# Making the first pair of token blocks with eight plain block products while the weights' sums are made, in a one-core hybrid pooling and attention block

## The chip, the cores and the metric

One core of one Trainium2 chip runs the whole block. The metric is the device time of one execution in microseconds (us). TensorE (PE) multiplies, VectorE (DVE), ScalarE (ACT) and GpSimd (POOL) do the elementwise work, and SyncE (SP) issues the DMAs.

## The reference

For 4096 tokens of width 1024 the block computes the following. The part that this change is about is the first line and the products with the columns of `w_in` that make v (attention values) and the attention gate.

```python
h = rms_norm(x, norm_gain)                       # (4096, 1024)
proj = h @ w_in                                  # (1024, 3072): pool_v, pool_g, q, k, v, attn_g
y_pool = multiscale_pool(pool_v, pool_w, pool_scale) * silu(pool_g)
y_attn = chunked_rel_attention(q, k, v, rel_bias) * silu(attn_g)
x = x + concat(y_pool, y_attn) @ w_out
out = rms_norm(x, final_norm_gain)
```

## The kernel before

The program has three phases that follow one another on every engine: the h phase (`h_phase_pe` and its sisters), the q phase (pool path and queries and keys) and the a phase (attention and output). The change lies in the h phase.

The h phase takes the 32 blocks of 128 tokens in 16 pairs p = 0 to 15. For each block it loads x, squares it (ACT, `square`), takes the root (POOL, `rstd`), normalises it (DVE, `normalise`) and transposes it on PE (`transposes(n)`, n = 2p or 2p+1, eight matmuls of 128x128 fp32). Every fp32 operand and every weight is split into two f16 parts, a high one made by ACT (`operand_hi`, `sum_hi`, `weight_hi`) and a low one, the rest, made by DVE (`operand_lo`, `weight_lo`) or, for sums of operands, by POOL (`sum_lo`). A pair times the 1024x1024 weights (columns of v and of the gate) is a product of 2x2 blocks of matrices. It is done with seven block products instead of eight (a Strassen-like scheme): `product(p, s)`, s = 0 to 6, twelve matmuls of 128x512 f16 each. The price is sums: four sums of operands per pair (DVE, `sums`), and, once, four sums of the weight quadrants W11, W12, W21, W22. DVE makes these four in halves of 128x1024 fp32 (`weight_s1`, `weight_sum`), and seven weights are split in halves (`weight_hi`, `weight_lo`), so product 1 can't start until DVE has summed, ACT has made the high part and DVE the low part. The results are taken out of PSUM by DVE (`take_u2`, `take_u4`, `take_c22`, `take_c12`, `take_c21`, `take_c11_lo`) and ACT (`copy_p1`, `v11_hi`), and stored.

The order of instructions on each engine is written out by hand: a list for the first pair(s) and then a loop over p. All engines issue in order, so an instruction that waits holds up everything behind it on its engine. In the loop, DVE does `take_c21(p - 1)` and `normalise(2p + 2)` first, and PE does `transposes(2p + 2)` after product 1 of pair p. In the four pairs of `FOLD_AT` PE does extra work beside the products (`fold_transposes`, `fold_products`): it folds the small pool weights into columns of w_in. In the pair after each, ACT, DVE and POOL split the folded weights (`group_hi`, `group_lo`, `group_sums`). In pair 3 DVE also makes the rows of the bias (`bias_rows`).

Of the kernel before, what the change touches and what calls it, by code (L numbers as in the profile page):

```python
# [65 lines left out]
FOLD_AT = (1, 4, 7, 10)  # L66
# [33 lines left out]
def build(nc, x, norm_gain, w_in, pool_w, pool_scale, rel_fwd, rel_rev, w_out, final_gain, out):  # L100
# [13 lines left out]
    with ctx:  # L114
# [3 lines left out]
        def sem(name):  # L118
# [90 lines left out]
        names = """ident0 ident_ready consts log_ready inv_ready ones_ready gain_loaded pw_loaded small_loaded  # L209
            w_hi w_lo s1_done sum_done wst_loaded fold_t fold_copied fold_mm fold_done fs_done  # L210
            ss_done ms_done rstd_done xn_done tr_done hhi_done hlo_done b12_done t_done th_done tl_done h_stored
# [6 lines left out]
        z_stored = [sem(f"h_z_stored{s}") for s in range(2)]  # L218

        def h_phase_pe(pe):  # L220
# [48 lines left out]

            def product(p, s):  # L270

                if p == 0:
                    pe.wait_ge(H["w_lo"], 2 * s + 2)
# [3 lines left out]
                if s == 0:  # L277
                    at_least(pe, H["c11_lo"], p)
                elif s < 4:
                    at_least(pe, H["u_done"], 5 * (p - 1) + (1, 4, 5)[s - 1])  # L280
                elif s == 4:
                    pe.wait_ge(H["p1_done"], p + 1)
                else:
                    pe.wait_ge(H["u_done"], 5 * p + s - 3)
# [11 lines left out]
            transposes(1)  # L296
            for p in range(PAIRS):
                for s in range(PRODUCTS):
# [9 lines left out]
                    elif p + 1 < PAIRS:  # L308
                        if s == (4 if p == 0 else 1):
                            transposes(2 * p + 2)  # L310
                        if s == (5 if p == 0 else 3):
                            transposes(2 * p + 3)
# [8 lines left out]
        def w_source(s, half):  # L321

            kts = slice(2 * half, 2 * half + 2)
            return (wraw[:, 0, kts, :], wsum[:, 1, kts, :], wsum[:, 0, kts, :], wsum[:, 2, kts, :], wraw[:, 1, kts, :],
                    wsum[:, 0, kts, :], wraw[:, 3, kts, :])[s]

        def h_phase_act(act):
# [11 lines left out]
            def weight_hi(s, half):  # L339

                if s in (0, 4, 6):
                    act.wait_ge(wraw_loaded[2 * {0: 0, 4: 1, 6: 3}[s] + half], 16)
                elif s == 2:
                    act.wait_ge(H["s1_done"], half + 1)
                else:
                    act.wait_ge(H["sum_done"], {1: 0, 3: 2, 5: 4}[s] + half + 1)
                nc.scalar.activation(wvg[:, s, 0, 2 * half:2 * half + 2, :], w_source(s, half), ACT.Copy,
                                     scale=WS).then_inc(H["w_hi"], 1)

# [14 lines left out]
            def sum_hi(p, i):  # L364

                act.wait_ge(H["t_done"], 4 * p + i + 1)
                nc.scalar.activation(hop1[:, p % 2, (2, 1, 3, 6)[i], 0, :], tsum[:, i, :], ACT.Copy).then_inc(H["th_done"], 1)

            def copy_p1(p):
                act.wait_ge(H["prod_mm"], PRODUCTS * p + 1)  # L370
                at_least(act, H["u_done"], 5 * (p - 1) + 1)
                nc.scalar.activation(u1[:, 0, :], pj[0][:, :], ACT.Copy, scale=1 / WS).then_inc(H["p1_done"], 1)

            def v11_hi(p):
                act.wait_ge(H["prod_mm"], PRODUCTS * p + 5)
# [7 lines left out]
            def v12_hi(p):  # L383
                act.wait_ge(H["u_done"], 5 * p + 4)
# [5 lines left out]
            def gate_tanh(p, e):  # L390

                act.wait_ge(H["u_done"], 5 * p + (3 if e else 5))
# [15 lines left out]
            def group_hi(i, j):  # L408

                s, src = parts_of_group(j)  # L410
                if j == 0:
                    act.wait_ge(H["w_lo"], 14)
                    if i == GROUPS - 1:
                        act.wait_ge(H["ext_stored"], 16)
# [7 lines left out]
            weight_hi(0, 1)  # L422
            operand_hi(0, 0)
            operand_hi(0, 1)
            copy_b12(0)
            operand_hi(0, 2)
            sum_hi(0, 0)
            sum_hi(0, 1)
            weight_hi(1, 0)
            weight_hi(1, 1)  # L430
            sum_hi(0, 2)
            sum_hi(0, 3)
            weight_hi(2, 0)
            weight_hi(2, 1)
            copy_p1(0)
            weight_hi(3, 0)
            weight_hi(3, 1)
            square(2)
            weight_hi(4, 0)
            weight_hi(4, 1)  # L440
            square(3)
            weight_hi(5, 0)
            weight_hi(5, 1)
            weight_hi(6, 0)
            weight_hi(6, 1)
            v11_hi(0)
            operand_hi(1, 0)
            operand_hi(1, 1)
            square(4)
            copy_b12(1)  # L450
            operand_hi(1, 2)
            for i in range(4):
                sum_hi(1, i)
            gate_tanh(0, 1)
            square(5)
            v12_hi(0)
# [37 lines left out]
        def h_phase_dve(dve):  # L494
# [3 lines left out]
            def weight_s1(half):  # L498

                kts = slice(2 * half, 2 * half + 2)  # L500
                dve.wait_ge(wraw_loaded[4 + half], 16)
                dve.wait_ge(wraw_loaded[6 + half], 16)
                nc.vector.tensor_tensor(wsum[:, 0, kts, :], wraw[:, 2, kts, :], wraw[:, 3, kts, :],
                                        ALU.add).then_inc(H["s1_done"], 1)

            def weight_sum(which, half):

                kts = slice(2 * half, 2 * half + 2)
                a11, a12, a21 = wraw[:, 0, kts, :], wraw[:, 1, kts, :], wraw[:, 2, kts, :]
                if which == 2:  # L510
                    dve.wait_ge(wraw_loaded[half], 16)
                    dve.wait_ge(H["s1_done"], half + 1)
                    ins = nc.vector.tensor_tensor(wsum[:, 1, kts, :], wsum[:, 0, kts, :], a11, ALU.subtract)
                elif which == 3:
                    ins = nc.vector.tensor_tensor(wsum[:, 2, kts, :], a11, a21, ALU.subtract)
                else:
                    dve.wait_ge(wraw_loaded[2 + half], 16)
                    dve.wait_ge(H["sum_done"], half + 1)
                    dve.wait_ge(H["w_lo"], 4 + half + 1)
                    ins = nc.vector.tensor_tensor(wsum[:, 0, kts, :], a12, wsum[:, 1, kts, :], ALU.subtract)  # L520
                ins.then_inc(H["sum_done"], 1)

            def weight_lo(s, half):
                dve.wait_ge(H["w_hi"], 2 * s + half + 1)
                nc.vector.scalar_tensor_tensor(  # L525
                    out=wvg[:, s, 1, 2 * half:2 * half + 2, :], in0=w_source(s, half), scalar=WS,
                    in1=wvg[:, s, 0, 2 * half:2 * half + 2, :], op0=ALU.mult, op1=ALU.subtract).then_inc(H["w_lo"], 1)

# [37 lines left out]
            def take_u2(p):  # L566
                dve.wait_ge(H["prod_mm"], PRODUCTS * p + 2)
                dve.wait_ge(H["p1_done"], p + 1)
                at_least(dve, H["u_done"], 5 * p)
                combine(u1[:, 1, :], pj[1], u1[:, 0, :])  # L570

            def take_u4(p):
                dve.wait_ge(H["prod_mm"], PRODUCTS * p + 3)
                dve.wait_ge(H["u_done"], 5 * p + 1)
                combine(u1[:, 2, :], pj[2], u1[:, 1, :])

            def take_c22(p):
                dve.wait_ge(H["prod_mm"], PRODUCTS * p + 4)
                dve.wait_ge(H["u_done"], 5 * p + 2)
# [28 lines left out]
            def group_lo(i, j):  # L608
                s, src = parts_of_group(j)
                dve.wait_ge(H["w_hi"], 14 + 7 * i + j + 1)  # L610
# [4 lines left out]
            def bias_rows():  # L615
# [5 lines left out]
                dve.wait_ge(H["w_lo"], 14)  # L621
# [10 lines left out]
            weight_lo(0, 0)  # L632
            normalise(1)
            weight_lo(0, 1)
            operand_lo(0, 0)
            operand_lo(0, 1)
            sums(0)
            operand_lo(0, 2)
            for half in range(2):
                weight_s1(half)  # L640
                weight_sum(2, half)
            for s in (1, 2):
                weight_lo(s, 0)
                weight_lo(s, 1)
            for half in range(2):
                weight_sum(3, half)
            take_u2(0)
            weight_lo(3, 0)
            weight_lo(3, 1)
            take_u4(0)  # L650
            weight_lo(4, 0)
            weight_lo(4, 1)
            for half in range(2):
                weight_sum(4, half)
            normalise(2)
            weight_lo(5, 0)
            take_c22(0)
            weight_lo(5, 1)
            normalise(3)
            weight_lo(6, 0)  # L660
            weight_lo(6, 1)
            take_c11_lo(0)
            operand_lo(1, 0)
# [1552 lines left out]
```

## Time and profile before

| | |
|---|---|
| time, median of 3 runs | 1685.61 us (1684.76 to 1685.9) |
| the profiled execution's own time | 1687.45 us |
| its span, first to last instruction | 1685.7 us |
| PE busy | 1618.0 us (96%) |
| DVE, ACT, POOL busy | 1064.6, 835.5, 691.8 us |
| mean granted TensorE clock | 0.988 of full |

The span is what the trace shows. The h phase fills about its first 365 us. "Busy" of PE counts overlapping matmuls, so two matmuls that start 0.2 us apart and take 0.38 us each show as continuous work.

### The profile page before, as it was taken

How to read it: one execution, taken by the hardware profiler on the slowest of the kernel's cores; microseconds unless marked ns; L12 is line 12 of the kernel's file. 1: busy time of each engine (PE TensorE's matmuls, PEld its weight loads, DVE VectorE, ACT ScalarE, POOL GpSimd, SP SyncE). 2: the span in 40 equal slices, each digit the busy share in tenths (PEclk: the TensorE clock that was granted, in tenths of full speed). 3: DMA queues.
4: the chain of work that ended last, by engine and by line, in shares of the span. 5: the costliest groups of instructions: out<-in, count | busy, mean ns of one | idle time of the engine just before them, and what ended most of it. 6: DMA issues, size and time to landing. Idle time of an engine off the chain costs nothing. (4 is left out here: it accounts for less than half of the span.)

```text
span 1685.7 us, 44263 instructions
## 1 busy us (share of the span) xinstructions
PE 1618.0 (96%) x17920; PEld 1219.7 (72%) x17920; DVE 1064.6 (63%) x2188; ACT 835.5 (50%) x1580; POOL 691.8 (41%) x734
## 2 busy tenths in 40 slices
PE   4999999999999999999988999999999999999986
PEld 2545545558677776777767888889888899888864
DVE  7777677647565566557346666666666666666664
ACT  5655555422121111112125677767777767777674
POOL 2545445311101111112413555555555555555553
PEclk8999999999999999999998999999999999999998
DMA  5564664564524532452854524444334444344331
GB/s 212 204 232 166 202 234 162 216 245 150 212 68 172 198 147 79 176 189 98 232 186 131 154 85 134 139 141 140 119 103 133 146 139 144 87 134 132 104 123 51
DMA packets 131201, 257.87 MB, mean 153 GB/s; under 512 B 15512, under 2 KB 61096, under 8 KB 128952
## 3 DMA queue, kind: packets, MB, share of 16 engines
q1 hardware_dynamic: 129960, 253.74, 44.7%
q8 instruction: 143, 2.34, 0.6%
q0 software_dynamic: 1040, 1.31, 0.4%
q14 instruction: 58, 0.48, 0.1%
HBM read 151.33 MB, written 83.48 MB: 139 GB/s over the span
## 5 line engine op out<-in xcount | busy, mean ns | idle before, releaser
L2092 POOL TENSOR_TENSOR stages<-stages 128x512 f16<-128x512 f32 (+2 forms) x368 | 364.0, 991 | 366.4 <-ACT stages L1929 366.2
L1561 PE MATMUL bank<-middle,weights 128*128 128x128 f16 x1792 | 313.2, 220 | 2.1 <-DVE entry L1208 0.9
L1564 PE MATMUL bank<-middle,weights 128*128 128x128 f16 x1792 | 313.1, 220 | 0.0
L1563 PE MATMUL bank<-middle,weights 128*128 128x128 f16 x1792 | 313.0, 220 | 0.0
L1923 ACT ACTIVATE stages<-bank,log_ps 128x512 f32<-128x512 f32 (+2 forms) x368 | 221.6, 602 | 161.9 <-PE bank L1816 97.0
L1763 DVE CUSTOM_DVE_ANT_0 stages<-bank,stages 128x640 bf16<-128x640 f32 (+4 forms) x256 | 198.7, 776 | 76.0 <-PE bank L1728 75.8
L977 PE MATMUL bank<-middle 128*128 128x256 f16 x784 | 213.7, 273 | 3.7 <-DVE stages L1117 3.7
L979 PE MATMUL bank<-middle 128*128 128x256 f16 x784 | 213.7, 273 | 0.0
L980 PE MATMUL bank<-middle 128*128 128x256 f16 x784 | 213.7, 273 | 0.0
L1929 ACT ACTIVATE stages<-stages 128x512 f16<-128x512 f32 (+2 forms) x368 | 202.8, 551 | 11.7
L1793 PE MATMUL bank<-entry,stages 128*128 128x512 f16 x768 | 193.3, 383 | 2.5 <-DVE stages L1984 2.5
L289 PE MATMUL bank<-weights,middle 128*128 128x512 f16 x448 | 172.2, 384 | 10.3 <-DVE weights L525 10.3
L1561 PEld LDWEIGHTS bank<-middle,weights 128*128 128x128 f16 x1792 | 176.1, 98 | 3.3 <-issue 1.3
L1563 PEld LDWEIGHTS bank<-middle,weights 128*128 128x128 f16 x1792 | 176.2, 98 | 0.4
L1564 PEld LDWEIGHTS bank<-middle,weights 128*128 128x128 f16 x1792 | 176.2, 98 | 0.0
L292 PE MATMUL bank<-weights,middle 128*128 128x512 f16 x448 | 171.8, 383 | 0.0
L291 PE MATMUL bank<-weights,middle 128*128 128x512 f16 x448 | 171.6, 383 | 0.0
L1001 PE MATMUL bank<-entry,stages 128*128 128x512 f16 x768 | 171.3, 382 | 0.0
L1813 PE MATMUL bank<-middle 128*128 128x256 f16 (+1 forms) x840 | 162.4, 243 | 2.8 <-DVE middle L2016 1.6
L1283 POOL TENSOR_TENSOR stages<-stages 128x512 f16<-128x512 f32 x32 | 38.2, 1194 | 300.0 <-ACT stages L1062 300.0
L1001 PEld LDWEIGHTS bank<-entry,stages 128*128 128x128 f16 x768 | 75.3, 98 | 86.7 <-issue 2.3
L1594 DVE SCALAR_TENSOR_TENSOR middle<-bank,middle 128x256 f32<-128x256 f32 x160 | 67.8, 424 | 103.2 <-PE bank L1564 102.0
(147 smaller groups left out, 3613.0 us busy)
## 6 DMA issues: line engine op xcount, KB each, us to landing
entry<-in_x SPq DMA_DIRECT2D x64, 512.0 KB, 3.7
h_ops<-middle SPq DMA_DIRECT2D x16, 1792.0 KB, 6.1
middle<-h_ops SPq DMA_DIRECT2D x112, 256.0 KB, 6.0
middle<-h_ops SPq DMA_DIRECT2D x49, 512.0 KB, 7.1
middle<-middle SPq DMA_DIRECT2D x384, 64.0 KB, 2.0
residual<-entry SPq DMA_DIRECT2D x32, 512.0 KB, 2.8
entry<-residual SPq DMA_DIRECT2D x30, 512.0 KB, 5.4
out<-entry SPq DMA_DIRECT2D x30, 512.0 KB, 2.6
```

The source lines that it names most:

```text
L977: nc.tensor.matmul(bank, wh, hop[:, :, s, 0, kt, :], start=(kt == 0 and s < 4), stop=False, skip_group_check=True)
L979: nc.tensor.matmul(bank, wh, hop[:, :, s, 1, kt, :], start=False, stop=False, skip_group_check=True)
L980: mm = nc.tensor.matmul(bank, wl, hop[:, :, s, 0, kt, :], start=False, stop=(kt == 3), skip_group_check=True)
L1001: mm = nc.tensor.matmul(op_bank(n, n2), part, w[:, kt, n2 * 512:(n2 + 1) * 512], start=(kt == 0 and w is wot_h and part is yh), stop=(kt = ...
L1561: nc.tensor.matmul(dst, wh, hop3[:, o, 0, kt, :], start=(kt == 0 and s < 2 and pair == 0), stop=False, skip_group_check=True)
L1563: nc.tensor.matmul(dst, wh, hop3[:, o, 1, kt, :], start=False, stop=False, skip_group_check=True)
L1564: mm = nc.tensor.matmul(dst, wl, hop3[:, o, 0, kt, :], start=False, stop=(kt == 3), skip_group_check=True)
L1763: nc.vector.tensor_tensor_reduce((junk0 if t == 0 and h < 2 else junk2)[:, c:640], wide[:, c:640], bias_q[:, h, c:640], 1.0, -3e38, ALU.ad ...
L1793: mm = nc.tensor.matmul(out_bank(t, i), yh, w, start=(m == 0), stop=(m == 11))
L1923: nc.scalar.activation(p32[g][:, a:b], score_bank(g)[:, a:b], ACT.Exp, bias=log_ps[:, 0:1]).then_inc(A["exp_done"], 1)
L1929: nc.scalar.activation(p_h[:, h % 2, c + a:c + b], p32[g][:, a:b], ACT.Copy).then_inc(A["ph_done"], 1)
L2092: nc.gpsimd.tensor_tensor(p_l[:, h % 2, c + a:c + b], p32[g][:, a:b], p_h[:, h % 2, c + a:c + b], ALU.subtract).then_inc(A["pl_done"], 1)
```

## The change

The first pair (p = 0) no longer uses the sums. It is made by eight products of plain quadrants (`FIRST`: weight, place of the operand, PSUM bank), two into each of four banks. The quadrants are put where splits 0, 4, 5 and 6 of the seven lie (`WSPLITS`); split 5 is overwritten later by its sum. Each bank then holds a result, which DVE takes out with one multiplication (`first_take`). The sums are made in the meantime and are needed from pair 1 on: two of them (W21+W22 and W11-W21, two halves each) by POOL instead of DVE, the other two by DVE. Eight weights are split instead of seven. The second operand quadrant of block 0 gets a split of its own (`first_b12_hi`, `first_b12_lo`). Transposes 1, 2 and 3 stand among the eight products. The gain is loaded before the first weights, W12 before W21 and W22. Everything of pair 1's operands and of the second, third and fourth normalise stands at new places in the lists. The folds move from pairs 1, 4, 7, 10 to 2, 5, 8, 11, and with them the splits from pairs 2, 5, 8, 11 to 3, 6, 9, 12; `bias_rows` stays in pair 3. The first columns of the folded group are loaded after the stores of pair 0.

```diff
-FOLD_AT = (1, 4, 7, 10)
+FIRST = ((0, 0, 0), (1, 4, 0), (0, 6, 1), (1, 5, 1), (2, 0, 2), (3, 4, 2), (2, 6, 3), (3, 5, 3))
+WSPLITS = (0, 4, 5, 6, 1, 2, 3, 5)
+FOLD_AT = (2, 5, 8, 11)
...
+            def first_product(q):
+                w, place_, role = FIRST[q]
+                if place_ == 6:
+                    pe.wait_ge(H["b12_lo"], 1)
+                else:
+                    pe.wait_ge(H["hlo_done"], {0: 1, 4: 2, 5: 3}[place_])
+                for kt in range(4):
+                    if kt % 2 == 0:
+                        pe.wait_ge(H["w_lo"], 2 * w + kt // 2 + 1)
...
             def product(p, s):
-                if p == 0:
-                    pe.wait_ge(H["w_lo"], 2 * s + 2)
+                if p == 1 and s in (1, 2, 3, 5):
+                    pe.wait_ge(H["w_lo"], {1: 10, 2: 12, 3: 14, 5: 16}[s])
...
             transposes(0)
-            transposes(1)
-            for p in range(PAIRS):
+            for q in range(len(FIRST)):
+                first_product(q)
+                if q == 0:
+                    transposes(1)
+                if q == 5:
+                    transposes(2)
+                if q == 6:
+                    transposes(3)
+            for p in range(1, PAIRS):
...
             def weight_hi(w, half):
+                if w == 7:
+                    act.wait_ge(H["prod_mm"], 6)
+                    act.wait_ge(H["w_lo"], 6)
...
+            def first_take(which):
+                dve.wait_ge(H["prod_mm"], 2 * which + 1)
+                nc.vector.tensor_scalar(cs1[:, which - 1, :], pj[which][:, :], 1 / WS, None,
+                                        ALU.mult).then_inc(H["u_done"], 1)
...
+            for half in range(2):
+                weight_sum(7, half)
+                weight_lo(7, half)
             gate_z(0, 1)
-            take_c12(0)
...
+            def weight_sum(w, half):            # POOL
+                kts = slice(2 * half, 2 * half + 2)
+                pool.wait_ge(wraw_loaded[4 + half], 16)
+                if w == 5:
+                    pool.wait_ge(wraw_loaded[6 + half], 16)
+                    ins = nc.gpsimd.tensor_tensor(wsum[:, 0, kts, :], wraw[:, 2, kts, :], wraw[:, 3, kts, :], ALU.add)
+                else:
+                    pool.wait_ge(wraw_loaded[half], 16)
+                    ins = nc.gpsimd.tensor_tensor(wsum[:, 2, kts, :], wraw[:, 0, kts, :], wraw[:, 2, kts, :], ALU.subtract)
```

On POOL, the rows that follow the second `rstd` of the program stood so before (L721 is `sum_lo`, L712 and L714 are `rstd`):

```order
16 L721 TENSOR_TENSOR middle<-entry,middle 128x512 x4
17 L712 TENSOR_TENSOR stat<-stat,eps 128x1
18 L714 TENSOR_TENSOR stat<-stat,pow_half 128x1
19 L712 TENSOR_TENSOR stat<-stat,eps 128x1
20 L714 TENSOR_TENSOR stat<-stat,pow_half 128x1
```

At the same place of the changed kernel (L778 and L781 are the new `weight_sum`, L788 is `sum_lo`, L766 and L768 are `rstd`):

```order
17 L778 TENSOR_TENSOR middle<-middle 128x1024 x2
18 L766 TENSOR_TENSOR stat<-stat,eps 128x1
19 L768 TENSOR_TENSOR stat<-stat,pow_half 128x1
20 L781 TENSOR_TENSOR middle<-middle 128x1024
21 L788 TENSOR_TENSOR middle<-entry,middle 128x512 x2
22 L766 TENSOR_TENSOR stat<-stat,eps 128x1
23 L768 TENSOR_TENSOR stat<-stat,pow_half 128x1
24 L788 TENSOR_TENSOR middle<-entry,middle 128x512
25 L781 TENSOR_TENSOR middle<-middle 128x1024
```

So four additions of 128x1024 have come in ahead of and between the `sum_lo` of pair 0.

On DVE, the end of the written-out list before, from the last weight splits (L525 is `weight_lo`) to `normalise(4)` (L535; L542 is `operand_lo`, L549 to L559 are `sums`, L604 is `gate_z`, L563 the takes, L585 `take_c11_lo`):

```order
27 L525 SCALAR_TENSOR_TENSOR weights<-middle,weights 128x1024 x2
28 L585 SCALAR_TENSOR_TENSOR stages<-bank,stages 128x512
29 L542 TENSOR_TENSOR middle<-bank,middle 128x512 x2
30 L549 SCALAR_TENSOR_TENSOR entry<-bank,entry 128x512
31 L554 TENSOR_TENSOR entry<-bank,entry 128x512
32 L556 TENSOR_TENSOR entry<-bank,entry 128x512
33 L559 TENSOR_TENSOR entry<-bank,entry 128x512
34 L542 TENSOR_TENSOR middle<-bank,middle 128x512
35 L604 SCALAR_TENSOR_TENSOR stages<-stages 128x512
36 L563 SCALAR_TENSOR_TENSOR stages<-bank,stages 128x512 x2
37 L535 SCALAR_TENSOR_TENSOR entry<-entry,stat 128x1024
```

The same stretch of the changed kernel, to its `normalise(4)` (L589; L566 is `weight_lo`, L596 `operand_lo`, L580 `first_take`, L560 the last `weight_sum`, L658 `gate_z`):

```order
25 L596 TENSOR_TENSOR middle<-bank,middle 128x512
26 L566 SCALAR_TENSOR_TENSOR weights<-middle,weights 128x1024 x2
27 L580 TENSOR_SCALAR stages<-bank 128x512
28 L566 SCALAR_TENSOR_TENSOR weights<-middle,weights 128x1024 x2
29 L560 TENSOR_TENSOR middle<-middle 128x1024
30 L566 SCALAR_TENSOR_TENSOR weights<-middle,weights 128x1024
31 L560 TENSOR_TENSOR middle<-middle 128x1024
32 L566 SCALAR_TENSOR_TENSOR weights<-middle,weights 128x1024
33 L658 SCALAR_TENSOR_TENSOR stages<-stages 128x512
34 L589 SCALAR_TENSOR_TENSOR entry<-entry,stat 128x1024
```

Three of the splits now stand after the operands of pair 1 and ahead of `normalise(4)`, the last of them each behind its own sum.

## Rows read from the trace of the kernel before

**Rows 1.** The page, section 1: busy time, share of the span, instructions.
```profile
PE 1618.0 (96%) x17920; PEld 1219.7 (72%) x17920; DVE 1064.6 (63%) x2188; ACT 835.5 (50%) x1580; POOL 691.8 (41%) x734
```

**Rows 2.** Stretches: length, busy us by engine (instructions), PE's granted clock, DMA share, GB/s.
```profile
20.10:27.60 7.50, 0.97 (x4) 0.25 (x2) 7.29 (x6) 3.37 (x5) 0.94 (x2) 0.75 0.20 48
27.60:30.40 2.80, 2.74 (x7) 1.03 (x8) 2.04 (x3) 2.16 (x3) 2.80 (x2) 0.50 0.00 0
30.40:37.20 6.80, 4.42 (x19) 1.62 (x18) 6.80 (x7) 4.16 (x6) 1.16 (x3) 0.98 0.64 270
37.20:40.60 3.40, 3.40 (x10) 1.23 (x9) 3.40 (x4) 1.92 (x3) 1.80 (x2) 0.54 0.00 0
...
360.00:400.00 40.00, 40.00 (x332) 32.30 (x331) 22.18 (x49) 7.86 (x17) 3.44 (x3) 1.00 0.75 279
```

**Rows 3.** What PE waited for in the first 330 us: total, times, longest.
```profile
PE bank L241 <- DVE entry L535: 18.8, 6, 9.3
PE bank L289 <- DVE weights L525: 10.3, 3, 6.6
PE bank L241 <- ACT stages L404: 1.2, 1, 1.2
```

**Rows 4.** Timeline of PE: start, length, what; the first matmuls of pairs 1 to 5.
```profile
48.79 1.04 PE L241 MATMUL bank<-ident,entry 128*128 128x128 f32 x8
49.66 0.38 PE L289 MATMUL bank<-weights,middle 128*128 128x512 f16 x1
...
52.26 0.38 PE L289 MATMUL bank<-weights,middle 128*128 128x512 f16 x1
...
76.24 0.38 PE L289 MATMUL bank<-weights,middle 128*128 128x512 f16 x1
...
97.92 0.38 PE L289 MATMUL bank<-weights,middle 128*128 128x512 f16 x1
...
117.80 0.38 PE L289 MATMUL bank<-weights,middle 128*128 128x512 f16 x1
...
140.35 0.38 PE L289 MATMUL bank<-weights,middle 128*128 128x512 f16 x1
```

**Rows 5.** Timeline of DVE, four places: first and fifth normalise, splits, bias rows.
```profile
8.00 1.28 DVE L535 SCALAR_TENSOR_TENSOR entry<-entry,stat 128x1024 f32<-128x1024 f32 x1 [8.00 <-DMA entry<-in_norm_gain]
...
28.36 3.43 DVE L525 SCALAR_TENSOR_TENSOR weights<-middle,weights 128x1024 f16<-128x1024 f32 x2 [0.76 <-ACT weights L347]
...
57.80 1.27 DVE L535 SCALAR_TENSOR_TENSOR entry<-entry,stat 128x1024 f32<-128x1024 f32 x1
...
117.65 2.52 DVE L629 TENSOR_SCALAR middle<-stages 8x575 f32<-8x575 f32 x6
```

**Rows 6.** Timeline of POOL in the first pair.
```profile
26.94 3.77 POOL L721 TENSOR_TENSOR middle<-entry,middle 128x512 f16<-128x512 f32 x2 [6.56 <-ACT middle L367]
...
39.20 2.92 POOL L712 TENSOR_TENSOR stat<-stat,eps 128x1 f32<-128x1 f32 x1 [1.60 <-ACT entry L336]
```

**Rows 7.** Timeline of POOL in pair 2, the sums of a folded group.
```profile
81.33 1.72 POOL L740 TENSOR_TENSOR stages<-stages 128x512 f32<-128x512 f32 x1
```

**Rows 8.** Timeline of DVE beside it.
```profile
81.84 1.75 DVE L611 SCALAR_TENSOR_TENSOR middle<-stages,middle 128x512 f16<-128x512 f32 x1
83.52 0.68 DVE L563 SCALAR_TENSOR_TENSOR stages<-bank,stages 128x512 f32<-128x512 f32 x1
```

**Rows 9.** Groups of the first 345 us: busy, mean ns, idle before and its end.
```profile
L721 POOL TENSOR_TENSOR middle<-entry,middle 128x512 f16<-128x512 f32 x61 | 70.8, 1193 | 67.9 <-ACT middle L367 67.9
L563 DVE SCALAR_TENSOR_TENSOR stages<-bank,stages 128x512 f32<-128x512 f32 x73 | 49.4, 683 | 42.8 <-PE bank L292 42.8
L525 DVE SCALAR_TENSOR_TENSOR weights<-middle,weights 128x1024 f16<-128x1024 f32 x14 | 17.8, 1291 | 0.8 <-ACT weights L347 0.8
L515 DVE TENSOR_TENSOR middle<-middle 128x1024 f32<-128x1024 f32 x2 | 2.3, 1212 | 0.0
```

**Rows 10.** Timeline of ACT: the second square and a weight's high part.
```profile
11.07 1.06 ACT L336 ACTIVATE entry<-entry 128x1024 bf16<-128x1024 f32 x1 [3.87 <-DMA entry<-in_x]
...
12.12 1.04 ACT L347 ACTIVATE weights<-middle 128x1024 f16<-128x1024 f32 x1
```

More of the change, by code:

```diff
@@ L366, in sum_hi @@
                 act.wait_ge(H["t_done"], 4 * p + i + 1)
+                if p == 0 and i == 3:
+                    act.wait_ge(H["prod_mm"], 6)
+                    act.wait_ge(H["b12_lo"], 1)
                 nc.scalar.activation(hop1[:, p % 2, (2, 1, 3, 6)[i], 0, :], tsum[:, i, :], ACT.Copy).then_inc(H["th_done"], 1)
@@ L438, in h_phase_act @@
             square(2)
+            for i in range(3):
+                sum_hi(0, i)
+            square(3)
             weight_hi(4, 0)
             weight_hi(4, 1)
-            square(3)
+            operand_hi(1, 0)
+            operand_hi(1, 1)
+            sum_hi(0, 3)
             weight_hi(5, 0)
             weight_hi(5, 1)
[L444 to L449, printed above, removed]
             copy_b12(1)
             operand_hi(1, 2)
-            for i in range(4):
+            for i in range(3):
                 sum_hi(1, i)
+            weight_hi(6, 0)
+            sum_hi(1, 3)
+            weight_hi(6, 1)
+            square(4)
+            v12_hi(0)
+            weight_hi(7, 0)
+            weight_hi(7, 1)
+            square(5)
             gate_tanh(0, 1)
-            square(5)
-            v12_hi(0)
             for p in range(1, PAIRS):
@@ L821, in h_phase_sp @@
             load_x(0)
+            sp.dma_start(gain[:, :], norm_gain[0:1, :].to_broadcast([P, D])).then_inc(H["gain_loaded"], 16)
             load_w(0, 0)
-            sp.dma_start(gain[:, :], norm_gain[0:1, :].to_broadcast([P, D])).then_inc(H["gain_loaded"], 16)
+            load_x(1)
             load_w(0, 1)
-            load_x(1)
+            for half in range(2):
+                load_w(1, half)
             for half in range(2):
@@ L828, in h_phase_sp @@
                 load_w(3, half)
-            for half in range(2):
-                load_w(1, half)
             load_x(2)
@@ L837, in h_phase_sp @@
             sp.dma_start(rel[:, 1, :], rel_rev).then_inc(H["small_loaded"], 16)
+            store_v(0, 0)
+            load_x(4)
             store_h(0)
-            load_x(4)
-            load_group(0)
             load_x(5)
-            store_v(0, 0)
-            store_z(0, 1)
             store_h(1)
             store_v(0, 1)
+            store_z(0, 1)
+            load_group(0)
             for p in range(1, PAIRS):
```

201 lines of the change are left out of this document (108 added, 93 removed).

## Prediction

> **What bounds the kernel now.** I read the page first: PE is busy 96% of the span [rows 1], so a change counts by what it does to PE's path. At the seam to the q phase, 360 to 400 us, PE is busy all 40.00 us at clock 1.00 [rows 2], so what the h phase gains or loses is handed on whole. Then I asked what PE waits for in the h phase: 18.8 us for a normalise (9.3 of it the start), 10.3 us for a weight's low part, 1.2 us for ACT [rows 3]. The stretches show where: between 20.1 and 27.6 us PE is busy 0.97 us and DVE 7.29 of 7.50, and from 30.4 to 37.2 DVE is busy 6.80 of 6.80 [rows 2]. The first pair is bound by DVE. The same rows show PE's clock at 0.50 just after the idle and at 0.54 again after the next one; 2.8 and 3.4 us at about half speed cost some 1.4 and 1.6 us.
>
> The marks on PE: pair 0's products end and pair 1 starts at 52.26, pair 2 at 76.24, pair 3 at 97.92, pair 4 at 117.80, pair 5 at 140.35 [rows 4]. A product takes 52.26 - 49.66 = 2.60, a little less (2.58) undisturbed; a block's transposes 49.66 - 48.79 = 0.87. The plain pair 3 takes 19.88, pair 4 with a fold 22.55, pair 2 with the splits 21.68. So a fold costs PE 2.67 and the splits 1.8.
>
> **What the reader should follow is DVE, not PE.** In the changed order PE has its eight products early, but transposes(4) stands after product 1 of pair 1 and needs normalise(4), row 37 of DVE's list before and row 34 now. PE issues in order: five products of pair 1 are behind it. Before, normalise(4) starts at 57.80 [rows 5], while PE reaches transposes(4) three products and a fold's transposes after 52.26, at 52.26 + 7.8 + 0.9 = 60.9, without a wait.
>
> **DVE's time up to normalise(4), before.** Prices are the group's means less the 0.08 by which the next one overlaps, and less what lies in waits: 1024-wide ones 1.14 (the sum L515 1.212, 1.27 for a normalise, taken as 1.20), 512-wide ones 0.60 (L563 0.683) [rows 5, 9]. Work: 4 normalise 4.8, 14 weight_lo 16.0, 8 halves of sums 9.1, 6 operand_lo 3.6, 8 sums 4.8, 6 takes 3.6, 1 gate_z 0.6: 42.5. Start 8.00. That leaves 57.8 - 50.5 = 7.3 for waits and for what the next paragraph is about.
>
> **POOL and DVE block each other.** Two weight_lo that should take 2.4 take 3.43 at 28.36, where POOL's two sum_lo take 3.77 instead of 2.3 [rows 5, 6]. In pair 2 a POOL sum of 128x512 takes 1.72, not the 1.19 of the L721 group [rows 9], and the DVE split beside it 1.75 instead of 0.68, while the DVE take next to it, which reads PSUM and one SBUF operand, keeps its 0.68 [rows 7, 8]. So a POOL addition and a DVE operation with two SBUF operands take turns: each waits until the other's whole instruction is over. The Trainium skill's page "SBUF — State Buffer", section "SBUF: two separate sides", says so: the pair of ports is an exclusive lock held for a full instruction, and DVE takes part with two SBUF inputs; by it a POOL instruction twice as long blocks DVE twice as long, and the sum comes out as below. The rule speaks against this change, and no 1024-wide addition on POOL is in the trace of before.
>
> **The change on DVE.** Removed: 4 halves of sums (-4.6), 6 takes become 4 (-1.2). Added: 2 weight_lo (+2.3), first_b12_lo (+0.6). Work 42.5 - 2.9 = 39.6, with small dependencies 40.
> Start: the gain lands one transfer earlier. Transfers land some 1.8 apart here, so 8.00 becomes 6.3 [rows 5], and x of block 1, now fourth and not fifth, comes at about 9.7 instead of 11.07 [rows 10].
> Waits that I find by laying the two lists side by side with these prices: W11's first half now lands at 8.0 and needs its high part of 1.04 [rows 10], DVE waits 1.3; operand_hi stands behind square(1), 1.2; first_b12 needs transposes(1), which stand behind the whole of product 0 and so behind W11's second half, 1.9; each half of the last weight is a sum on DVE, a high part on ACT, a low part on DVE with nothing between, 2 x 1.15; the tanh 0.4. Together 7.1.
> POOL: no row has a 1024-wide addition. Its length is put at 2.3, twice the 1.19 of a 512-wide one [rows 9] less one start; at least 1.2, if the length hardly grew with the columns, and at most 3.4, twice the 1.72 of [rows 7], if that were its own length and no wait. 2.3 is taken because 1.72 stands beside DVE's 1.75, so both hold a wait. Walking POOL's list beside DVE's, the second one (W21+W22, second half, 19.5 to 22.0) stops a weight_lo for 1.5, the fourth (W11-W21, second half) one for 2.1; the eight sum_lo of pairs 0 and 1, which now meet weight splits and normalises instead of PSUM reads, cost 0.4 to 1.05 in seven places, 5.7. Together 9.3. Before, the like places cost about 2 (1.0 of it in the row at 28.36 [rows 5]).
> Sum: 6.3 + 40 + 7.1 + 9.3 = 62.7, against 57.80. Normalise(4) ends at about 64.0 and PE's transposes(4) start near 64.3, after 13 us in which PE has nothing (it has pair 0 done by about 43 and product 1 of pair 1 by 51).
>
> **From there to the end.** Pair 2 starts at 64.3 + 2 x 0.87 + 5 x 2.58 + 1.8 for a PE that starts at half clock after the idle (between the 1.4 and 1.6 seen [rows 2] and one more product at half speed) = 80.7. Before 76.24: +4.5. That the eighth product (2.58) and the earlier start do not appear is no oversight: they lie in time that PE spends waiting.
> The fold: pair 1 had it before 76.24; now it is in pair 2, after this mark. From pair 2 on there are four folds instead of three: +2.7. The splits, four times 1.8, are behind the mark in both.
> The bias rows: 2.52 us of DVE [rows 5], until now in a pair without splits, with slack. Now they follow the last split of pair 3, and normalise(10) is behind them. Before, the normalise that followed a splits pair ended 0.4 us before PE needed it, so some 2 of them are seen: +1.8. The bounds are 0 (the splits of pair 3 run with more slack) and 2.5.
> Sum: 4.5 + 2.7 + 1.8 = +9.0. The profiled span 1685.7 becomes 1694.7, its own time 1687.45 becomes 1696.4. The median, which stands 1.8 below that execution, 1685.6 + 9.0 = 1694.6.
> SP's queue: load_group(0) now waits for store_z(0, 1), so for gate_z(0, 1) at 62; its group is needed at pair 2's fold_transposes, after 83. Hidden by 20 us. The load of block 6 is behind it, and square(6) with it is some 2 us late, without a waiter. inv_count, 30 small memsets, stays in pair 2. ACT gets two more high parts (2.1), under DVE's time.
>
> **Rivals.**
> (a) PE gets what the edit offers: if normalise(4) were ready by 45, PE would do eight products, three transposes and pair 1 without the 13 us: pair 2 at about 64, -12, and with fold and bias -8: 1678. For it: PE's waits and slow clock of the first pair are some 13 us. Against: DVE has 40 us of work ahead of normalise(4) however the rest goes, and starts at 6.3, so 46 is the floor with no wait at all. It decides from normalise(4) before 50. Chance 0.05.
> (b) The port costs little: POOL's long additions fall beside PSUM reads, or DVE goes ahead of POOL. The latter has a row: a one-element POOL operation took 2.92 at 39.20 while DVE went from one instruction to the next [rows 6]. With DVE always first its stalls are about 5.5 and pair 2 starts near 77, in all +5. With none at all, pair 2 at 71.5 and -0.2: same. +5 belongs to my forecast's range; the chance of within 3.4 us is 0.13.
> (c) The POOL additions take 3.4 and hold DVE for it: 6 more, 1701. Chance 0.12.
> (d) My forecast, DVE late by about 5 and two later terms, +5 to +12: 0.70.
>
> **How the numbers follow.** A measurement of this kernel can tell 0.2%, 3.4 us. Faster 0.05 from (a), same 0.13 from (b), slower 0.82 from (c) and (d). Range: down to the light port, 1688.5, up to the long additions, 1700.5; it leaves out about 2 in 10.
>
> **What would show it.** The changed trace should have the first product near 12 to 13 us, pair 1's product 0 between 40 and 46, one wait of PE of 9 to 15 us for a normalise after pair 1's product 1, POOL's 1024-wide additions above 2.2 us, weight_lo of 2 us and more beside them, pair 2's start at 77 to 84, and a wait of 1 to 2.5 us in pair 4 behind the bias rows. I'd be wrong if normalise(4) came before 57.8, or if POOL's long additions left DVE's lengths alone.

## The result, and the profile after

The changed kernel takes 1689.81 us (median of 11 runs, 1687.41 to 1695.18), the kernel before 1685.22 us (11 runs, 1680.82 to 1686.96). The ratio is 1.003 with a 95% interval of 1.0017 to 1.0042, that is 2.9 to 7.1 us slower. The forecast was 1694.6, or 9.0 us slower: the direction and the range hold, the size is too large. The profiled execution took 1688.93 us with a span of 1687.1.

The page, section 1, against [rows 1], and PE's waits in the first 330 us, against [rows 3]:

```profile
PE 1618.1 (96%) x17932; PEld 1220.0 (72%) x17932; DVE 1067.1 (63%) x2185; ACT 837.1 (50%) x1582; POOL 704.6 (42%) x738
```

```profile
PE bank L251 <- DVE entry L589: 30.4, 9, 12.8
PE bank L320 <- DVE middle L596: 2.3, 1, 2.3
PE bank L293 <- DVE middle L596: 1.6, 1, 1.6
PE bank L293 <- DVE weights L566: 0.2, 1, 0.2
```

The 10.3 us in which PE waited for the low parts of weights are down to 0.2. In their place the wait for a normalise has grown from 18.8 to 30.4, with one piece of 12.8. PE's timeline shows where (first matmuls of pairs 0 to 5 and 15, and the transposes that waited):

```profile
11.65 0.61 PE L293 MATMUL bank<-weights,middle 128*128 128x512 f16 x1 [1.65 <-DVE middle L596]
...
42.60 0.61 PE L320 MATMUL bank<-weights,middle 128*128 128x512 f16 x1 [2.32 <-DVE middle L596]
...
63.00 1.97 PE L251 MATMUL bank<-ident,entry 128*128 128x128 f32 x8 [12.80 <-DVE entry L589]
...
79.34 0.38 PE L320 MATMUL bank<-weights,middle 128*128 128x512 f16 x1
...
101.89 0.38 PE L320 MATMUL bank<-weights,middle 128*128 128x512 f16 x1
...
113.80 1.09 PE L251 MATMUL bank<-ident,entry 128*128 128x128 f32 x8 [0.51 <-DVE entry L589]
...
122.50 0.38 PE L320 MATMUL bank<-weights,middle 128*128 128x512 f16 x1
...
129.35 1.09 PE L251 MATMUL bank<-ident,entry 128*128 128x128 f32 x8 [1.51 <-DVE entry L589]
...
144.11 0.38 PE L320 MATMUL bank<-weights,middle 128*128 128x512 f16 x1
...
356.28 0.38 PE L320 MATMUL bank<-weights,middle 128*128 128x512 f16 x1
```

Pair 1 starts 9.7 us earlier than before (42.60 against 52.26 in [rows 4]), pair 2 starts 3.1 us later (79.34 against 76.24). All of the lead is lost in the one wait that ends at 63.00. The granted clock is at half from 52.60 to 66.30, that is during this wait and for 3.3 us after it (and once before, for 3.4 us, from 42.4):

```profile
52.60:66.30 13.70, 3.30 (x12) 2.31 (x13) 8.97 (x10) 5.98 (x9) 3.94 (x5) 0.50 0.60 215
```

(Columns as in [rows 2]: PE busy 3.30 of 13.70 us, granted clock 0.50.) DVE, from the first normalise to `normalise(4)`, against [rows 5]:

```profile
6.70 1.28 DVE L589 SCALAR_TENSOR_TENSOR entry<-entry,stat 128x1024 f32<-128x1024 f32 x1 [6.70 <-DMA entry<-in_norm_gain]
...
20.08 6.19 DVE L566 SCALAR_TENSOR_TENSOR weights<-middle,weights 128x1024 f16<-128x1024 f32 x4
...
36.47 5.48 DVE L566 SCALAR_TENSOR_TENSOR weights<-middle,weights 128x1024 f16<-128x1024 f32 x2
...
46.87 3.66 DVE L566 SCALAR_TENSOR_TENSOR weights<-middle,weights 128x1024 f16<-128x1024 f32 x2
...
61.66 1.28 DVE L589 SCALAR_TENSOR_TENSOR entry<-entry,stat 128x1024 f32<-128x1024 f32 x1
```

and POOL beside it, against [rows 6]; L781 is the new `weight_sum` (W11-W21), L788 `sum_lo`:

```profile
25.51 2.98 POOL L781 TENSOR_TENSOR middle<-middle 128x1024 f32<-128x1024 f32 x1
...
35.42 3.35 POOL L781 TENSOR_TENSOR middle<-middle 128x1024 f32<-128x1024 f32 x1
38.73 2.14 POOL L788 TENSOR_TENSOR middle<-entry,middle 128x512 f16<-128x512 f32 x1
45.07 6.46 POOL L788 TENSOR_TENSOR middle<-entry,middle 128x512 f16<-128x512 f32 x4 [4.21 <-ACT middle L415]
```

Two `weight_lo` that alone would take 2.4 us take 5.48 at 36.47, where a 1024-wide sum and a `sum_lo` run, and 3.66 at 46.87 beside four `sum_lo`. The group of all sixteen `weight_lo` in the first 82 us has a mean of 1614 ns; before, it was 1291 ns over fourteen [rows 9]. Taken instruction by instruction up to normalise(4), over the lengths that each has where nothing stands beside it (1.22, 1.28 and 0.68 us), DVE lost 2.2 us in the kernel before and about 9.1 in the changed one. Such lost time is called a stall below.

```profile
L566 DVE SCALAR_TENSOR_TENSOR weights<-middle,weights 128x1024 f16<-128x1024 f32 x16 | 25.2, 1614 | 3.3 <-ACT weights L388 3.3
```

### The profile page after: what moved, and what is told of

It is laid out like the page before. It is cut to its first block and busy times, and to the rows that moved or that the text cites. A ratio compares the mean times of both kernels' runs of the same rounds, so it can differ in the third digit from the quotient of the medians.

```text
span 1687.1 us, 44293 instructions
## 1 busy us (share of the span) xinstructions
PE 1618.1 (96%) x17932; PEld 1220.0 (72%) x17932; DVE 1067.1 (63%) x2185; ACT 837.1 (50%) x1582; POOL 704.6 (42%) x738
## 5 line engine op out<-in xcount | busy, mean ns | idle before, releaser
L1050 PE MATMUL bank<-middle 128*128 128x256 f16 x784 | 213.7, 273 | 2.3 <-DVE stages L1190 2.3
L320 PE MATMUL bank<-weights,middle 128*128 128x512 f16 x420 | 160.3, 382 | 2.8 <-DVE middle L596 2.3
L322 PE MATMUL bank<-weights,middle 128*128 128x512 f16 x420 | 160.1, 381 | 0.0
L323 PE MATMUL bank<-weights,middle 128*128 128x512 f16 x420 | 159.9, 381 | 0.0
```

Source lines behind the costliest of these rows:

```text
L1050: nc.tensor.matmul(bank, wh, hop[:, :, s, 0, kt, :], start=(kt == 0 and s < 4), stop=False, skip_group_check=True)
```

## The experiments

Times are medians against runs of the kernel before on the same chip. "Mark" is the start of a pair's first matmul on PE, as in [rows 4]. Marks of one kernel differ from execution to execution; two kernels were therefore profiled again.

**e6 and e7: the kernel before and the changed one, profiled again.** No edit.

> The kernel before once more, for a second trace. If the recovery behind the first phase (the shift is 6.44 us at 331 us and 1.5 us at the end, in the two traces) belongs to the change, this trace has the half clock window at 853 us again. If it is chance of the granted clock, its half clock windows between 640 and 910 us lie elsewhere and its last mark differs from that of the first trace by some us, with the first phase the same within 1 us.

> The changed kernel once more, for a second trace, with the same question: its first phase should end 5 to 7 us after that of the kernel before, whatever the rest does. Pair 2 starts at 79 to 81.5.

e6: 1683.62 us, span 1681.8, pair 2 at 75.48, pair 15 at 349.05 (in the trace of before 76.24 and 349.84). e7: 1690.82 us, span 1689.0, PE's wait 12.79 until 63.70, pair 2 at 80.38, pair 15 at 357.35. Four executions have the changed kernel's order up to pair 2 (the first, e3, e7, and e8, which differs there only by POOL's memsets in pair 1): PE goes on at 63.00, 64.23, 63.70 and 64.11, pair 2 starts at 79.34, 81.18, 80.38 and 80.92, mean 80.5. Two have the order before, mean 75.9. So pair 2 is 4.6 us later, and the first trace, with 3.1, was the luckiest of the four. The four differ from the start on: PE's clock rises from half to full (its matmuls start 0.43 us apart, then 0.22) at 15.1 us in the first trace, at 17.5, 16.5 and 17.1 in e3, e7 and e8, and DVE waits 1.1, 2.4, 1.7 and 2.2 us for `first_b12`, whose high part on ACT stands behind transposes(1) on PE. The later the rise, the longer this wait and the later pair 2. Marks of one trace are good to about 1 us here, and the readings below use both.

The traces also show that less than the shift at pair 15 reaches the end. PE's waits from 600 to 920 us, where the q phase goes over into the a phase, e6 first:

```profile
PE bank L1728 <- DVE m L1763: 6.2, 5, 2.4
PE bank L1728 <- DMA middle<-middle: 2.7, 1, 2.7
PE bank L977 <- DVE stages L1117: 2.6, 3, 2.1
```

and e7:

```profile
PE bank L1801 <- DVE m L1836: 6.0, 5, 2.4
PE bank L1801 <- DMA middle<-middle: 1.8, 1, 1.8
PE bank L1050 <- DVE stages L1190: 1.7, 3, 1.3
```

The DMA row and the row of L977 (L1050 in the changed kernel) are 0.9 us shorter each. The shift between these two traces is 8.3 us at pair 15 and 7.2 at the end (spans 1681.8 and 1689.0), so 1.1 is given back; between the first two traces it is 6.4 and 1.4, so 5.0 is given back. That PE comes later is not enough to explain it. The span less the mark of pair 15 is 1335.8 in the trace of before, 1332.8 in e6, 1334.9 in e10 and 1336.9 in e4, the four traces with the folds in pairs 1, 4, 7, 10. It is between 1327.3 (e3) and 1332.5 (e2) in the nine with the folds in 2, 5, 8, 11, and among these are e5, e9 and e11 (1330.9, 1328.2, 1331.5), whose pair 15 (349.89, 347.25, 350.32) is hardly later than in the kernel before (349.84 and 349.05). The means of the two groups are 4.5 us apart. The DMA row and the L977 row together come to 3.3 to 4.9 us in the nine, to 5.3 to 6.3 in the three traces with the old first pair (before, e6, e10), and to 4.5 in e4. So with the change the rest of the program seems to run some us shorter, late or not. No experiment was made for this, and the profiled execution of e4 is the slowest of its ten: the cause stays open.

**e1: POOL's sums left out.** What is left out of the computation: W21+W22 and W11-W21 are not formed, weights that need them are split from raw quadrants, so products with them have other values. Everything else runs as before. With the sums the waits for them go too, but DVE's waits for high parts of weights are 3.3 us in both kernels, and in neither does it wait for POOL's sums.

```diff
-            weight_sum(5, 0)
-            weight_sum(5, 1)
             rstd(2)
-            weight_sum(6, 0)
...
-            weight_sum(6, 1)
             sum_lo(0, 3)
```

> The two sums of weights on GpSimd are left out: the weights of splits 2 and 3 are made from the raw quadrants W22 and W21 and the other sums from them, so products 2 and 3 of pairs 1 to 15 have other values; all other work stays. Lock theory (the long GpSimd additions stop VectorE for whole instructions): no weight_lo over 2.3 us before 45 us, normalise(4) about 4 us earlier than the 61.66 of the changed kernel, pair 2 starts at 75 to 76.5 instead of 79.34. Rival (GpSimd's sums cost VectorE nothing on its path, the delay is VectorE's own work and its waits): normalise(4) and pair 2 within 0.5 us of 61.66 and 79.34. The end of the span moves by less than the mark of pair 2 if the seams behind the first phase take up part of it.

1686.33 us (10 runs), ratio 1.0004 (0.9988 to 1.002). PE's transposes(4) and the group of `weight_lo`:

```profile
58.11 1.97 PE L251 MATMUL bank<-ident,entry 128*128 128x128 f32 x8 [11.12 <-DVE entry L589]
```

```profile
L566 DVE SCALAR_TENSOR_TENSOR weights<-middle,weights 128x1024 f16<-128x1024 f32 x16 | 21.6, 1382 | 3.4 <-ACT weights L388 3.3
```

PE goes on 4.9 us earlier than in the first trace of the changed kernel and pair 2 starts at 75.29, as the lock theory said, 4.1 us earlier (5.2 against the mean of four). DVE executes the same instructions; the sixteen splits alone are 16 x 0.232 = 3.7 us shorter. All of DVE's stalls up to normalise(4) fall from 9.1 to 3.8 us, and normalise(4) starts at 56.78 instead of 61.66. So work given to POOL costs DVE about half of its own length here: four sums of 2.36 us (one of them undisturbed, in e3) cost about 5 us of DVE.

**e2: the same sums on DVE.** The four additions stand on DVE's list, each pair ahead of the splits that use it.

```diff
+            weight_sum(5, 0)
+            weight_sum(5, 1)
...
+            weight_sum(6, 0)
+            weight_sum(6, 1)
```

> The four half sums that GpSimd makes go to VectorE, which makes them behind normalise(2) and behind the operands of pair 1; nothing else changes. They cost VectorE 4 x 1.14 = 4.6 us. Theory A (GpSimd's additions block VectorE for about 4 us of its path): pair 2 starts at 79 to 82, that is no gain, 0 to 2.6 us later. Theory B (blocking is far worse than the work itself): pair 2 starts at 75 to 77. Theory C (blocking costs nothing): pair 2 starts 4 to 5 us later, at 84.

1695.0 us (4 runs), ratio 1.0067 (1.0041 to 1.0092), the slowest kernel of the study.

```profile
65.29 1.97 PE L251 MATMUL bank<-ident,entry 128*128 128x128 f32 x8 [16.59 <-DVE entry L601]
```

Pair 2 starts at 82.74: 3.4 us later than in the changed kernel's first trace, which is more than was expected of that comparison, and 2.3 later than the mean of four. DVE's stalls are 6.0 us instead of 9.1, and its work is 4.6 longer. By the marks GpSimd is the better place for the sums in spite of the lock; by time the intervals of the two kernels still touch (1.0041 and 1.0042).

**e3: the bias rows in pair 4.**

```diff
-BIAS_AT = 3
+BIAS_AT = 4
```

> The changed kernel with the rows of the bias in pair 4 (no splits) instead of pair 3. In the changed kernel pair 3 takes 20.61 and pair 4 21.61. Theory (the bias rows behind the last split of pair 3 hold up normalise(10)): pair 4 takes 19.9, the wait of PE near 127.5 us goes, pair 5 starts 1.7 us earlier. Rival (pair 4's wait comes from the splits of pair 3 alone): no change. In the time 1.7 us less at most, in the noise.

1688.06 us (10 runs), ratio 1.0015 (1.0003 to 1.0028). Pair 4 takes 19.88 us instead of 21.61, and PE has no wait in it: the term of 1.8 is 1.73. Pair 3 stays at 20.59. The gain in time, 1.0015 against 1.003, is within the intervals.

**e4: the folds a pair earlier.**

```diff
-FOLD_AT = (2, 5, 8, 11)
+FOLD_AT = (1, 4, 7, 10)
```

(and the load of the first group with them)

> The changed kernel with the folds in pairs 1, 4, 7, 10 as before and the group's columns loaded early. Theory (moving the fold out of pair 1 moved 2.7 us of PE work from a place with an idle PE to one without): pair 2 starts at about 78 to 81 in spite of the fold, since a fold's transposes and product 2 fit in the 12.8 us wait, and from pair 2 to the end of the phase there are three folds: pair 15 starts 2.5 to 4 us earlier than 356.28. Rival (the fold is not hidden in pair 1): pair 2 starts 2.7 us later, at 82, and pair 15 at 356.

1687.54 us (10 runs), ratio 1.0018 (1.0003 to 1.0034). The profiled execution took 1693.73, the slowest of the ten. Pair 15 starts at 355.01, 1.3 earlier than in the first trace of the changed kernel and 2.3 earlier than in e7; 2.5 to 4 was expected: missed. The fold does lie in the long wait, but pair 2 starts at 81.43, 2.1 later (0.9 by the mean). PE:

```profile
64.58 1.94 PE L251 MATMUL bank<-ident,entry 128*128 128x128 f32 x8 [10.73 <-ACT stages L448]
66.32 3.62 PE L276 MATMUL bank<-stages 128*128 128x128 f32 x16
```

and ACT in the same stretch:

```profile
62.35 0.63 ACT L443 ACTIVATE stages<-stages 128x512 f32<-128x512 f32 x1 [0.82 <-DVE stages L658]
62.89 0.58 ACT L421 ACTIVATE stages<-bank 128x512 f32<-128x512 f32 x1
63.37 1.07 ACT L448 ACTIVATE stages<-bank 128x512 f32<-128x512 f32 x2
```

ACT's copy of the folded transposes (L448) stands behind a tanh (L443) that waits for DVE's `gate_z`; normalise(4) was done at 63.45, and PE still waited until 64.58 for that copy. Then `fold_products` (L276, sixteen matmuls in 3.62 us) stands behind transposes(4), where nothing hides it. Work put into idle time brought a wait of its own, and only a part of its 2.67 us fitted. From pair 2 to pair 15 this kernel takes 273.58 us, the kernel before 273.60 and the changed one 276.94: the 3.4 us between them are the fold (+2.67), the bias rows, here again in a pair without splits (+1.73), and the changed kernel's shorter pair 3 (-1.07, see e8). The expectation had counted the fold alone.

**e5: normalise(4) ahead.** normalise(4) moves up before the last three weights' splits (5, 6 and 7), normalise(5) between the two halves of the last, ACT and POOL in the same order, the bias rows in pair 4.

```diff
+            normalise(4)
...
-            for half in range(2):
-                weight_sum(7, half)
-                weight_lo(7, half)
+            weight_sum(7, 0)
+            weight_sum(7, 1)
+            take_u2(1)
             gate_z(0, 1)
+            weight_lo(7, 0)
+            normalise(5)
+            weight_lo(7, 1)
```

> The changed kernel with another order: blocks 4 and 5 are squared, rooted and normalised ahead of or among the last splits of the weights, copy_p1(1) and take_u2(1) too, both halves of the last sum are made before their low parts (so ScalarE's part lies under VectorE's work), and the bias rows go to pair 4. Theory (PE waits for normalise(4) only because of its place in the list): the 12.8 us wait falls apart into waits of under 5 us for the splits, pair 2 starts at 70 to 73 instead of 79.34, the time falls by 6 to 9 us against the changed kernel, to about 1682, 3 us under the kernel before. Rival (VectorE's whole work of the first pairs is the bound, whatever its order): pair 2 starts at 76 or later.

1684.15 us (12 runs) against 1684.39 (17), ratio 0.9998 (0.9985 to 1.0011). PE in pair 1 and at pair 2:

```profile
52.62 0.39 PE L320 MATMUL bank<-weights,middle 128*128 128x512 f16 x1 [1.61 <-DVE weights L568]
...
61.61 1.19 PE L251 MATMUL bank<-ident,entry 128*128 128x128 f32 x8 [3.03 <-DVE entry L591]
...
74.69 0.38 PE L320 MATMUL bank<-weights,middle 128*128 128x512 f16 x1 [2.53 <-DVE stages L641]
```

In place of one wait of 12.8 us there are four of 0.4 to 3.0, and between 20 us and pair 2 PE's granted clock is at half for 3.4 us instead of 17.1; pair 2 starts 4.7 us earlier than in the first trace, 5.8 earlier than the mean of four. The expectation (70 to 73, and 1682) was too good: DVE has the same work in any order, and PE now waits for it at the splits, at a normalise and at `take_c11_lo` (L641). This order makes up for all that the change lost, and no more.

**e8: why pair 3 is short.** Pair 3 has the first splits and takes 20.61 us; the later pairs with splits take 21.66. The 30 memsets of `inv_count` on POOL stand between them and the sums of the group in pair 3 alone.

```diff
-                if p == 2:
+                if p == 1:
```

> The changed kernel with one difference: the 30 small memsets of inv_count, which POOL does in pair 2, stand in pair 1. Open point: pair 3 of the changed kernel, with the first splits of folded weights, takes 20.61 us, where the pairs with splits 6, 9 and 12 take about 21.66 (and pair 2 of the kernel before 21.68). Theory: the memsets occupy POOL for about 1 us right ahead of the sums of the group, so POOL's first sum starts behind DVE's first split instead of beside it, and does not block it. Without them in front, pair 3 should take 21.5 to 21.8, and pair 4 still 21.6. Rival: the first splits pair is shorter for another reason (the folded group of the first fold, the bias rows that come first on DVE): then pair 3 stays at 20.6. One profile is enough; the time should move by about 1 us, which is less than a single time can tell.

Pair 3 takes 21.68. The changed kernel, POOL's last memset and first sum (L807), and DVE's first split (L665) (PE's transposes were shown above: 113.80, wait 0.51):

```profile
107.96 0.10 POOL L856 MEMSET inv_count<- 128x1 f32 x1
108.02 1.29 POOL L807 TENSOR_TENSOR stages<-stages 128x512 f32<-128x512 f32 x1
```

```profile
107.50 0.68 DVE L665 SCALAR_TENSOR_TENSOR middle<-stages,middle 128x512 f16<-128x512 f32 x1
```

e8, POOL, DVE and PE:

```profile
108.57 1.72 POOL L807 TENSOR_TENSOR stages<-stages 128x512 f32<-128x512 f32 x1
```

```profile
109.08 1.75 DVE L665 SCALAR_TENSOR_TENSOR middle<-stages,middle 128x512 f16<-128x512 f32 x1
```

```profile
116.45 1.09 PE L251 MATMUL bank<-ident,entry 128*128 128x128 f32 x8 [1.59 <-DVE entry L589]
```

In e8 POOL's sum starts 0.51 us ahead of DVE's split, and the split takes 1.75 us. In the changed kernel it starts 0.52 us after the split's start, and the split takes 0.68. The difference of 1.07 is found again in PE's wait (1.59 against 0.51) and in the pair. e8 shows what [rows 7, 8] showed in the kernel before; the changed kernel has the cause switched off.

**e9: the gap in each splits pair, with e5's order.** The memsets are repeated in each fold pair. They compute nothing new; they delay POOL's sums by 1 us. The edit is against e5; the wait for the memsets in the q phase is raised to match.

```diff
-                if p == 2:
+                if p in FOLD_AT:
```

> The kernel of e5 with one difference: the 30 small memsets of inv_count are done again in each of the four fold pairs, so that each group's sums on POOL start about 1 us later. Theory (the same as for e8): each pair with splits is then about 1.07 us shorter, not only the first: pairs 6, 9 and 12 at 20.6 instead of 21.66, pair 15 starts at about 346.7 where e5 had 349.89, and the time is about 1681 against 1684.2 of e5 and 1684.4 of the kernel before, so a version below both kernels by about 0.2%. Rival 1: the shorter pair 3 has nothing to do with the memsets: pairs 6, 9 and 12 stay at 21.6 and the time is that of e5, 1684. Rival 2: the pairs become shorter, but what is gained is given back at the seams of the q phase: pair 15 at 346.7 and the time above 1683.

1681.81 us (10 runs) against 1686.75 (14), ratio 0.9974 (0.9961 to 0.9987). Pairs 3, 6, 9 and 12 take 20.60, 20.59, 20.58 and 20.61. POOL, DVE and PE in pair 6 and PE at pair 15:

```profile
166.65 1.29 POOL L815 TENSOR_TENSOR stages<-stages 128x512 f32<-128x512 f32 x1
```

```profile
166.13 0.68 DVE L667 SCALAR_TENSOR_TENSOR middle<-stages,middle 128x512 f16<-128x512 f32 x1
```

```profile
172.43 1.09 PE L251 MATMUL bank<-ident,entry 128*128 128x128 f32 x8 [0.49 <-DVE entry L591]
...
347.25 0.38 PE L320 MATMUL bank<-weights,middle 128*128 128x512 f16 x1
```

Pair 15 is 2.6 us earlier than in e5, by three times 1.07 less 0.6, of which 0.3 stand at the start of pair 2 and 0.3 in pair 7. This is the first kernel here whose interval lies below the kernel before.

**e10 and e11: is it the gap alone?** e10 is the kernel before with that one line changed (and the matching wait), e11 is e9 again beside it.

> The kernel before with one difference: the 30 small memsets of inv_count, done once in pair 2, are done in each of its fold pairs 1, 4, 7, 10, so that they stand ahead of each group's sums on POOL. It asks how much of e9's gain is the gap alone. Theory: the four pairs with splits, 2, 5, 8, 11, each fall from about 21.67 to 20.6, so pair 15 starts about 4.3 us earlier than before (near 345.3), and the time is 4 us below the kernel before, a ratio of about 0.9975; e9 (0.9974) is then worth no more than this, and the new first pair brings nothing even in its best order. Rival: in the order of the kernel before the gap helps less (its first splits are in pair 2, behind a pair of late operands), then pair 15 starts above 347 and the ratio is above 0.9985.

> The kernel of e9 once more, beside e10 on the same chip. If the two differ by no more than their intervals, the gap ahead of the group's sums is the whole of what is won. By the marks seen so far e5 stands level with the kernel before (pair 15 at 349.89 and 349.84 or 349.05), so the two should come out alike, both near 0.9975.

e10: 1681.74 us (12 runs) against 1686.12 (23), ratio 0.9977 (0.9961 to 0.9992); pairs 2, 5, 8, 11 take 20.59, 20.60, 20.58 and 20.60, pair 15 starts at 344.60, and from pair 2 to there it takes 3.9 us less than the kernel before (269.71 against 273.60). e11: 1683.47 (12 runs), ratio 0.9983 (0.9968 to 0.9999), pair 15 at 350.32, where PE waited 4.31 us at the start of pair 2 and then began it at half clock (pair 2 takes 25.32 us, in e9 22.55); in e9 that wait was 0.97. The intervals of e9, e10 and e11 overlap. One line in the kernel before gives what the whole new first pair gives in its best order plus that line, and the new first pair by itself gives nothing that these runs can tell.

## Why the prediction was right, and where it was off

**The bound and the place.** Right. PE did pair 0 early (first product at 11.65, a little ahead of the forecast 12 to 13; pair 1 at 42.60, forecast 40 to 46), and lost it in one wait for normalise(4) (12.8, forecast 9 to 15) because DVE's work up to there is what it was.

**DVE's sum.** Forecast 6.3 + 40 + 7.1 + 9.3 = 62.7, measured 61.66 in the first trace and 62.4 in the mean of the four. In the first trace the start was 6.70 (+0.4): the gain landed 1.3 us earlier than before, and not 1.7. The waits in DVE's row of waits are 3.3 for three high parts of weights, 1.1 for first_b12, 0.6 for operand_hi and 0.3 for the tanh, in all 5.3 (-1.8). The stalls, instruction by instruction over the undisturbed lengths, are 9.1 (-0.2). The rest is work, 61.7 - 6.7 - 5.3 - 9.1 = 40.6 (+0.6). The waits were over-sized: operand_hi behind square(1) cost 0.6 and not 1.2, W11's first half 1.05 and not 1.3. first_b12 cost 1.15 and not 1.9, but this was the first trace's luck: it is 1.7 to 2.4 in e7, e8 and e3. The stalls came out by two misses that cancel. The 1024-wide additions were forecast to stop DVE for 1.5 + 2.1 = 3.6; in the first trace they stopped it three times, for 0.9, 1.6 and 2.2, in all 4.7. The `sum_lo` were forecast at 5.7 and cost 4.4.

**The lock.** (The two engines blocking each other.) Right, and shown twice: e1 takes POOL's sums away and wins 4 to 5 us at pair 2 with DVE's instructions unchanged, e8 and e9 move the meeting of two instructions by 1 us and the 1.07 goes and comes. POOL's 1024-wide sum was put at 2.3; beside DVE it shows 2.98 and 3.35, undisturbed (in e3) 2.36. Rival (b), a cheap port, fell: it wanted stalls of 5.5 and pair 2 near 77, and the traces have 9.1 and 79.3 to 81.2. That its +5 lies next to the measured +4.6 is chance. Rival (c), 3.4 us that hold DVE for all of it, had the length in the record (3.35 at 35.42) but not the effect, since about 1.0 of that length (3.35 less 2.36) is POOL's own waiting.

**Pair 2.** Forecast +4.5: the first trace shows +3.1, the means of four and two executions +4.6. From the end of the wait to pair 2 PE took 16.3 to 17.0 us where the full clock would give 14.6: 1.7 to 2.3 for the half clock, forecast 1.8.

**Fold and bias rows.** +2.7 and +1.8 in the forecast, +2.67 (pair 2 takes 22.56 with its fold, a plain pair 19.88) and +1.73 (e3) in the traces.

**A step that failed: "inv_count, 30 small memsets, stays in pair 2"**, costed at nothing. It stays in pair 2, but the group's sums, which stood ahead of it, now come right behind it, in pair 3. That is -1.07, and e8 shows it. The list on each engine had been laid side by side up to normalise(4) and not at this place.

**"What the h phase gains or loses is handed on whole"** failed too. By marks the loss at pair 15 is 4.6 + 2.67 + 1.73 - 1.07 = 7.9 (6.4 between the first two traces, 8.3 between e6 and e7). Then 5.0 us of the first pair of traces' shift and 1.1 of the second's are given back by the end, in the mean 3.0. A part of it lies in PE's waits at the seams of the q phase, which are as short in e5, e9 and e11, where PE hardly comes late, as in the changed kernel (3.3 to 3.7 us against 3.5 and 4.2). One stretch of full PE at 360 to 400 us [rows 2] said nothing on what lies behind 640 us.

So the sum becomes +9.0 - 1.1 - 3.0 = +4.9, and the medians say +4.6, with an interval from 2.9 to 7.1. The agreement is no proof, since the 3.0 is the mean of two values 4 us apart: the trace of before has a stretch of half clock at 853 us that e6 has not. What shortens the rest of the program is not shown.

## What to carry to other kernels

Work moved off the bounding engine to GpSimd isn't free where both have SBUF operands: here it cost DVE about half of its length (normalise(4) 4.9 us later than in e1), which is still less than doing it on DVE (7.2 us later in e2, of which 4.6 are the work itself). Before filling the idle time of one engine, find what the instruction that ends it needs: PE's eight quick products, and the part of a fold that fitted beside them, did not bring pair 2 forward while normalise(4) stood behind all of DVE's splits. And look at which of two contending engines comes first at each meeting that repeats: 1 us of delay on POOL, in four places, was worth as much as anything that the large change could give.

## What the runs showed of the hardware

- The blocking between DVE and POOL depends on who comes first, even where the two start only about 0.5 us apart. A DVE split that starts 0.51 us after a POOL sum shows 1.75 us, one that starts 0.52 us before it shows 0.68, and POOL's sum then 1.29 instead of 1.72. The 30 memsets, which read nothing, did not lengthen the DVE instruction beside them (0.68 at 107.50).
- With both engines busy without a break they take turns, whole instructions at a time: two splits of 1.2 us take 5.48 us at 36.47 with one 1024-wide and one 512-wide POOL addition beside them. This isn't always so: the one-element POOL operation of [rows 6] at 39.20 took 2.92 us, and two whole DVE instructions of two SBUF operands ran within it.
- The same instructions up to pair 2 end within 1.8 us of each other in four executions (79.34 to 81.18), with the granted clock at 0.50 in stretches that lie a few us apart from one execution to the next (one begins at 52.6 in the first trace and at 54.7 in e8). They part early: PE's matmuls go from 0.43 to 0.22 us apart at 15.1 to 17.5 us, and DVE's wait for `first_b12` goes with it, from 1.1 to 2.4.
